# Expert tiles that add their rows to the residual stream, in place of a combine at the end

## What is computed

```python
t = rmsnorm(x, g_ffn)
g_logits, e_logits = t @ w_group + b_group, t @ w_router + b_router
g = argmax(g_logits)                       # one of 4 groups
top_v, top_i = top_k(e_logits[g], 2)       # 2 of its 4 experts
w = softmax(top_v) * softmax(g_logits)[g]
y = sum(w[k] * ((silu(t @ w_gate[e]) * (t @ w_up[e])) @ w_down[e]) for k, e in ...)
out = rmsnorm(x + y, g_final)
```

## Time and profile before

| | us |
|---|---|
| median of three runs (1074.95 to 1082.03) | 1076.79 |
| the profiled execution | 1083.94 |
| its span, first to last instruction | 1080.7 |
| routing, experts, combine | 69.5, 282.5, 59.7 |

### The profile page before, as it was taken

The page is one execution under the profiler, slowest core; times in us unless marked ns, Lnnn a source line. Parts: engine busy times, 40 slices in busy tenths (PEclk is TensorE's granted clock), DMA queues, the critical chain, the costliest instruction groups (busy, mean ns, idle before and its releaser), DMA issues. The chain is left out here.

```text
span 1080.7 us, 13980 instructions
## 1 busy us (share of the span) xinstructions
PE 943.3 (87%) x4765; PEld 764.4 (71%) x4765; DVE 431.6 (40%) x524; ACT 368.4 (34%) x544; POOL 128.6 (12%) x159
## 2 busy tenths in 40 slices
PE   6996999999999999989999997926999999989500
PEld 5785888888888676558888885715888887768400
DVE  4673212121211234232222232375646567675056
ACT  6762012111111123221122222503656567665212
POOL 0011000000001000000000001202112111211074
PEclk8997999999999999998999999965999999999855
DMA  9891101111005966544000102932587878993177
GB/s 384 329 297 60 49 1 39 40 40 40 20 20 210 408 262 279 203 182 161 1 1 1 29 1 76 331 118 79 196 309 260 307 260 317 341 337 131 69 268 259
DMA packets 37534, 181.38 MB, mean 168 GB/s; under 512 B 4268, under 2 KB 8748, under 8 KB 26811
## 3 DMA queue, kind: packets, MB, share of 16 engines
q1 hardware_dynamic: 26706, 141.57, 35.3%
q0 software_dynamic: 6864, 24.68, 7.2%
q10 hardware_dynamic: 3888, 14.16, 3.2%
HBM read 147.59 MB, written 40.78 MB: 174 GB/s over the span
## 5 line engine op out<-in xcount | busy, mean ns | idle before, releaser
L1634 DVE TENSOR_TENSOR Wl<-raw,Wh x48 | 109.9, 2292 | 72.9 <-ACT Wh L1574 72.8
L1574 ACT CAST Wh<-raw x48 | 91.6, 1911 | 55.4 <-issue 53.8
L1481 PE MATMUL ps<-Wh,e_xTh 128*128 x216 | 87.2, 404 | 4.0 <-issue 4.0
L551 PE MATMUL ps<-f_win_h,f_hTh 128*128 128x512 f32 x216 | 86.6, 401 | 0.6 <-DVE f_hTl L443 0.6
L1482 PE MATMUL ps<-Wl,e_xTh 128*128 x216 | 84.9, 393 | 0.0
L553 PE MATMUL ps<-f_win_l,f_hTh 128*128 128x512 f32 x216 | 84.8, 393 | 0.0
L1483 PE MATMUL ps<-Wh,e_xTl 128*128 x216 | 84.8, 393 | 0.0
L552 PE MATMUL ps<-f_win_h,f_hTl 128*128 128x512 f32 x216 | 84.5, 391 | 0.0
L1556 POOL DMA_INDIRECT e_xg<-h_rows,idx x28 | 46.7, 1669 | 247.0 <-PE ps L1666 199.3
L1481 PE MATMUL ps<-f_rg_h,f_cTh 128*128 128x512 f32 x144 | 56.7, 394 | 0.0
L1483 PE MATMUL ps<-f_rg_h,f_cTl 128*128 128x512 f32 x144 | 56.2, 390 | 0.0
(11 more groups left out here) (303 smaller groups left out, 1811.5 us busy)
## 6 DMA issues: line engine op xcount, KB each, us to landing
raw<-in_w_e SPq DMA_DIRECT2D x48, 1024.0 KB, 6.8
y_rows<-e_y ACTq DMA_DIRECT2D x27, 512.0 KB, 5.4
t_ring<-in_kc SPq DMA_DIRECT2D x8, 1024.0 KB, 12.5
t_ring<-in_vc SPq DMA_DIRECT2D x8, 1024.0 KB, 8.7
f_win_raw<-in_w_in SPq DMA_DIRECT2D x3, 2048.0 KB, 22.8
f_xin<-in_x SPq DMA_DIRECT2D x9, 512.0 KB, 3.6
x_rows<-f_xin SPq DMA_DIRECT2D x9, 512.0 KB, 2.6
y_rows<-in_x SPq DMA_DIRECT2D x1, 4608.0 KB, 19.8
```

Source lines behind the costliest of these rows:

```text
L551: pe.matmul(ps[:, bank, :], hTh[:, c, :], win_h[i][:, c, :], start=(c == 0), stop=False)
L1481: pe.matmul(out, xh, wh, start=(n == 0), stop=False)
L1574: act.copy(Wh[q][:, ds(off, PIECE)], raw[q][:, ds(off, PIECE)]).then_inc(hi_ok[q], 1)
L1634: dve.tensor_tensor(Wl[q][:, ds(off, PIECE)], raw[q][:, ds(off, PIECE)], Wh[q][:, ds(off, PIECE)].bitcast(F32), ALU.subtract).then_inc(lo_ ...
```

## The change

The combine goes. The stream is stored from `X` to `acc_rows` in DRAM at the end of routing. In the expert stage each tile gathers its rows of `acc_rows` (by the same `IDX`) into one of four slots `ring`; DVE adds `down`'s two halves to them out of PSUM; the weight of a pair (`GATE`) is already multiplied into `sg`. Rows that have one expert still to come are scattered back to `acc_rows` (`IDXR`), the others are squared by ACT, get their factor from POOL, are normed by DVE into `done` and scattered to the output `y` (`IDXF`). An index out of bounds drops a row, in the fetch too. To keep a row's two experts at least four tiles apart, the experts are numbered with the place in the group ahead of the group, and so are the weights in DRAM. The first four tiles have no norm. The last tile has its own tail: added, normed and scattered to `y` behind the loop. `xg` has three buffers instead of two and is filled with zeros by POOL at the start of routing; POOL's fetches run three tiles ahead.

The cut diff (the removed `combine_block`, declarations and host-side reshapes are left out):

```diff
-        for lo in range(MIN_TILES, NTILE, NT):
-            n = min(NT, NTILE - lo) * P
-            sp.dma_start(y_dram[lo * P:lo * P + n, :], io["x"][0:n, :]).then_inc(fill_st, 16)
-        sp.wait_ge(fill_st, 16 * -(-(NTILE - MIN_TILES) // NT))
...
@@ -1256,6 +1268,8 @@
                     for p in range(3):
                         sp.wait_ge(keep["w_ld"][p], 16 if n == 4 else 32)
                         load_piece(sp, io, keep, 1 if n == 4 else 2, p)
+            for n in range(NT):
+                sp.dma_start(acc_dram[n * P:(n + 1) * P, :], X[:, n, :]).then_inc(keep["acc_st"], 16)
             for b in range(XB):
...
         def _(pool):
             pool.memset(ones[:, :], 1.0).then_inc(ones_ok, 1)
+            pool.memset(keep["xg"][:, :, :], 0.0)
...
+                last = v(M[:, k, :, :].rearrange("p t (e g) -> p t e g", g=EG), bcast4(H[:, k, :, :], EG),
+                         G1[:, :, :].rearrange("p t (o g) -> p t o g", o=1).to_broadcast([P, NT, EE, EG]), ALU.mult)
             then(last)
             v(Ms[:, :, :], M[:, 0, :, :], M[:, 1, :, :], ALU.add).then_inc(M_ok, 1)
 
+
+            then(v(TK[:, 0, :], m["k1"][:, :], m["k2"][:, :], ALU.is_lt))
+            then(v(TK[:, 1, :], m["k2"][:, :], m["k1"][:, :], ALU.is_lt))
...
                 [P, K2, NTILE]), ALU.is_equal))
             for k in range(2):
-                last = v(A[:, k * NT:(k + 1) * NT, :], A[:, k * NT:(k + 1) * NT, :], bcast(tok[:, 0, :], NTILE), ALU.mult)
+                own = slice(k * NT, (k + 1) * NT)
+                then(v(A[:, own, 0, :], A[:, own, 1, :], bcast(TK[:, k, :], NTILE), ALU.mult))
+                last = v(A[:, own, 1, :], A[:, own, 1, :], bcast(WTr[:, k, :], NTILE), ALU.mult)
             last.then_inc(AB_ok, 1)
 
 
...
+            then(dve.tensor_scalar(none[:, :], val[:, :], 0.0, pad[:, :], ALU.is_equal, ALU.mult))
+            then(dve.scalar_tensor_tensor(out=none[:, :], in0=none[:, :], scalar=-1.0, in1=val[:, :], op0=ALU.add, op1=ALU.add))
+
+            dve.tensor_copy(IDX[:, :], none[:, :])
+            then(dve.scalar_tensor_tensor(out=val[:, :], in0=second[:, :], scalar=2 * LATER, in1=none[:, :], op0=ALU.mult,
+                                          op1=ALU.add))
+            then(dve.tensor_scalar(fin[:, :], second[:, :], -2 * LATER, 2 * LATER, ALU.mult, ALU.add))
+            dve.tensor_copy(IDXR[:, :], val[:, :])
+            then(v(fin[:, :], fin[:, :], none[:, :], ALU.add))
+            then(dve.tensor_copy(IDXF[:, :], fin[:, :]))
+            then(v(none[:, :], none[:, :], last_tile[:, :], ALU.mult))
+            then(r(used[:, 0:1], none[:, :], AX_X, ALU.add))
+            dve.tensor_copy(keep["idx_last"][:, :], used[:, 0:1])
 
 
 def split_product(pe, out, pairs):
...
+                if j >= XG:
+                    pool.wait_ge(tr_ps, j - XG + 1)
+                pool.indirect_dma_start(xg[:, j % XG, :], None, h_dram[:, :],
+                                        bass.IndirectOffsetOnAxis(ap=IDX[:, j:j + 1], axis=0), bounds_check=NT * P - 1, oob_is_err=False).then_inc(
+                    x_ld[j % XG], 16)
+
+            def gather(j):
+
+                if j >= EG:
+                    pool.wait_ge(y_st, 16 * (j - EG + 1))
                 else:
-                    with pool.If(started(pool, j - 1) >= 1):
-                        fetch(j)
+                    pool.wait_ge(acc_st, 16 * NT)
+                if j:
+                    pool.wait_ge(a_ld, 16 * j)
+                pool.indirect_dma_start(ring[:, j % 4, :], None, acc_dram[:, :],
+                                        bass.IndirectOffsetOnAxis(ap=IDX[:, j:j + 1], axis=0), bounds_check=NT * P - 1, oob_is_err=False).then_inc(a_ld, 16)
+
+            def scatter(j):
+                pool.wait_ge(y_ok, 2 * j + 2)
+                if j:
+                    pool.wait_ge(y_st, 16 * j)
+                pool.indirect_dma_start(acc_dram[:, :], bass.IndirectOffsetOnAxis(ap=IDXR[:, j:j + 1], axis=0),
+                                        ring[:, j % 4, :], None, bounds_check=NT * P - 1, oob_is_err=False).then_inc(y_st, 16)
+
+            def finish(j):
+
+                factors(j)
+                pool.wait_ge(f_ok, j - EG + 1)
+                if j > EG:
+                    pool.wait_ge(f_st, 16 * (j - EG))
+                pool.indirect_dma_start(io["y"], bass.IndirectOffsetOnAxis(ap=IDXF[:, j:j + 1], axis=0), done[:, j % 2, :],
+                                        None, bounds_check=SEQ + ROWS_S - 1, oob_is_err=False).then_inc(f_st, 16)
+
+            def factors(j):
+                c = 3 * (j % 2)
+                pool.wait_ge(sq_ok, SQ0 + j + 1)
+                pool.tensor_scalar(st[:, c + 1:c + 2], st[:, c:c + 1], 1.0 / D, EPS, ALU.mult, ALU.add).then_inc(r_ok, 1)
+                pool.wait_ge(r_ok, 2 * SQ0 + 2 * j + 1)
+                pool.tensor_tensor(st[:, c + 2:c + 3], st[:, c + 1:c + 2], nhalf[:, :], ALU.pow).then_inc(r_ok, 1)
+
+            pool.memset(factor[:, 0:1], 1.0 / D)
+            pool.memset(factor[:, 1:2], EPS)
+            for j in range(XG):
+                fetch(j)
+            with ExitStack() as maybe:
+                for s in range(NTILE):
+                    if s >= MIN_TILES:
+                        maybe.enter_context(pool.If(started(pool, s) >= 1))
+                    if s + XG - 1 < MIN_TILES:
+                        fetch(s + XG)
+                    elif s + XG < NTILE:
+                        with pool.If(started(pool, s + XG - 1) >= 1):
+                            fetch(s + XG)
+                    gather(s)
+                    if s >= 1:
+                        scatter(s - 1)
+                    if s > EG:
+                        finish(s - 1)
+
+            squares, before, every, added = squares_done(pool), sums(pool, 2), sums(pool, 3), sums(pool, 1)
+            pool.wait_ge(sq_ok, squares)
+            pool.tensor_tensor(mark[:, 1:2], mark[:, 0:1], factor[:, 0:1], ALU.mult).then_inc(mark_ok, 1)
+            pool.wait_ge(mark_ok, 1)
+            pool.tensor_tensor(mark[:, 1:2], mark[:, 1:2], factor[:, 1:2], ALU.add).then_inc(mark_ok, 1)
+            pool.wait_ge(mark_ok, 2)
+            pool.tensor_tensor(mark[:, 2:3], mark[:, 1:2], nhalf[:, :], ALU.pow).then_inc(mark_ok, 1)
+            pool.wait_ge(f_st, before)
+            pool.tensor_tensor(mark[:, 3:4], nhalf[:, :], nhalf[:, :], ALU.add).then_inc(mark_ok, 1)
+            pool.wait_ge(last_ok, 1)
+            pool.wait_ge(mark_ok, 4)
+            pool.indirect_dma_start(io["y"], bass.IndirectOffsetOnAxis(ap=keep["idx_last"][:, 0:1], axis=0), v_last,
+                                    None, bounds_check=SEQ + ROWS_S - 1, oob_is_err=False).then_inc(f_st, 16)
+
+            pool.wait_ge(f_st, every)
+            pool.tensor_tensor(mark[:, 3:4], nhalf[:, :], nhalf[:, :], ALU.add).then_inc(mark_ok, 1)
+            pool.wait_ge(y_st, added)
+            pool.wait_ge(mark_ok, 5)
+            pool.tensor_tensor(mark[:, 3:4], nhalf[:, :], nhalf[:, :], ALU.add).then_inc(mark_ok, 1)
 
         @block.scalar
         def _(act):
...
+            def square(j):
+                act.wait_ge(y_ok, 2 * j + 2)
+                act.wait_ge(sq_ok, SQ0 + j)
+                if j >= EG + 2:
+                    act.wait_ge(r_ok, 2 * (SQ0 + j) - 2)
+                    act.wait_ge(f_ok, j - EG - 1)
+                c = 3 * (j % 2)
+                act.activation(junk[:, :], ring[:, j % 4, :], ACT.Square, accum_out=st[:, c:c + 1]).then_inc(sq_ok, 1)
...
-                if like >= 1:
-                    par = (like - 1) % 2
-                    act.wait_ge(dn_ps, 2 * s - 1)
-                    if like >= 3:
-                        act.wait_ge(y_st[par], 8 * (s - 1 - par))
-                    act.copy(y[:, par, 0:512], ps[:, 4, :]).then_inc(y_ok, 1)
-                    act.wait_ge(dn_ps, 2 * s)
-                    act.copy(y[:, par, 512:D], ps[:, 5, :]).then_inc(y_ok, 1)
+                if like > EG:
+                    square(s - 1)
                 round_piece(s + 1, (2,))
-                if like >= 1:
-                    act.wait_ge(y_ok, 2 * s)
-                    act.dma_start(y_dram[ds((s - 1) * P, P), :], y[:, par, :]).then_inc(y_st[par], 16)
             tile_steps(act, step)
-
-            count = end(act, NE - 1)
-            stores = [act.value_load(TAB[0:1, 4, NE + par:NE + par + 1], min_val=16, max_val=8 * NTILE) for par in range(2)]
-            done = [tail(act, 1 + h) for h in range(2)]
-            act.wait_ge(y_st[0], stores[0])
-            for h in range(2):
-                act.wait_ge(dn_ps, done[h])
-                act.copy(y[:, 0, h * 512:(h + 1) * 512], ps[:, 4 + h, :]).then_inc(y_ok, 1)
-            act.wait_ge(y_ok, done[1])
-            act.dma_start(y_dram[ds((count - 1) * P, P), :], y[:, 0, :]).then_inc(y_st[0], 16)
-            act.wait_ge(y_st[0], stores[0] + 16)
-            act.wait_ge(y_st[1], stores[1])
-            act.copy(sg[0:1, 0:1], ident[0:1, 0:1])
+            every = tail(act, 2)
```

(36 more changed lines are left out.)

228 lines of the change are left out of this document (100 added, 128 removed).

## The result

The kernel before took 1080.12 us (median of 20 runs), the changed one 1074.53 us (median of 20): a ratio of 0.9947 with a 95% interval of 0.993 to 0.9963. That is a gain of 5.6 us where 20 were forecast. It is inside the range and within 1% of no change.

A forecast was written before the change was run, and what follows sets the result against it. PE was taken to bound the expert stage, with nothing running beside the 59.70 us combine. Terms -49.6 + 4.8 + 23 + 2 = -19.8 us took 1076.8 to 1057.0; range 1040 to 1068, 8 in 10 1036 to 1086.

The forecast's parts named there:

- behind the last matmul: End of the kernel: 59.7 us of combine shrink to a 10.1 us tail, -49.6 us.
- routing: Stage ahead of the experts: index path, index product, small operations behind it and POOL's fill add 4.8 us, bounds 3 and 8.
- first product to last: Expert stage, from first gate product on DVE to last: 250.75 us grow to 273.8, +23, bounds +9.5 and +31.
- 2 for the gather: Expert stage: a tile's gather is issued late in POOL's round and may land late, +2 us.
- step A: Expert step with two weight pieces on DVE: 9.9 with an early factor, 11.2 with a late one, 10.4 us taken.
- B: Expert step with one weight piece: additions, square, rounding, piece, norm, xTl and product in series, 10.3 us, nine of them.
- H: Expert step with three weight pieces: 11.3 us at least, 13.4 with a late factor, 12.9 taken, three with a norm.
- the first five: First five intervals between products, without a norm: three at PE's 9.3 us and two at 11, 49.9 together.
- The middle value: 10.4 us for a two-piece step, near the middle between POOL's scatter slipping ahead of the second piece and not.
- the rival that POOL is always late: Expert stage: every scatter generation meets a weight piece, stage +37 us, total -8, 1069 us; chance 0.15.
- Hidden work: Expert stage: PE keeps its pace because DVE catches up in one-piece steps; -45 us, 1032; chance 0.13.
- The round trip through memory: Expert stage: the loop of additions, scatter and gather binds; at 12.2 us per tile stage +55, total +11, 1088; chance 0.14.

The follow-up runs named there:

- round_early: Changed kernel with ACT's rounding of weight piece 0 of tile s+2 put ahead of the silu of tile s: 1061.57 us, 0.9833 of the kernel before.
- norm_next: Changed kernel with the norm of tile s-2 right behind the product of step s, its scatter to y one step later: 1047.62 us, 0.9705 of before.
- no_stream: Changed kernel without the gathers from and scatters to acc_rows in the expert loop: 1056.54 us, 0.9768 of the kernel before.
- factor_first: Changed kernel with POOL's two factor operations put ahead of the tile's scatter to acc_rows: 1056.94 us, 0.9791 of the kernel before.
- both: Changed kernel with the norm behind the next step's product and ACT's square behind the rounding of piece 2: 1041.79 us, 0.9635 of the kernel before.

## Why the prediction was right or wrong

The direction was right, the size was not: 20 us forecast, 5.6 measured. Against the sum's own terms, in the profiled executions:

| term | forecast | measured | from |
|---|---|---|---|
| behind the last matmul | -49.6 | -47.4 | 59.7 before, 12.3 now |
| routing | +4.8 | +3.7 | see below |
| ahead of routing | 0 | -2.4 | the same reduce of the attention ends 2.4 earlier |
| first product to last | +23, and 2 for the gather | +41.95 | 250.75, 292.70 |
| last product to last matmul | 0 | -1.9 | 13.65, 11.74 |
| sum | -19.8 | -6.1 | |

**The step that failed** is the cost of a step A, "9.1, under PE's 9.3" if the factor is early and "11.2" if it is late, from which 10.4 was taken. It measured 12.5. The working put the first piece right behind the product and left out the 1.81 us for which DVE waits there for ACT's rounding, though the earlier trace rows show that wait in the very row of 851.70. On the mean of the eight steps the rounding is waited for 1.84 us and the factor 1.83, and the rest of the step is 8.8, near the 9.1 of the sum: 10.4 left room for 1.3 us of waits where 3.7 were measured. The 11.2 has a slip besides: its 8.4 is counted from the start of the product, so the 0.41 at its end counts the product twice. Without that a late factor makes 10.8, and with the wait 12.6; with an early factor it is 10.9. Eight times 2.1 are 16.9 us, just what the stretch is off by. The others cancel, and that they do is luck (B +2.9, H -0.2, the first five -0.9, the last +0.2, no gather late -2). That the wait belongs to the chain is shown by `round_early`, which takes most of it away and 14.2 us with it, and by `norm_next`, which puts the norm into it and gains 24.

**The middle value was wrong as well.** The scatter was to slip ahead of the second piece half of the time. It never did: in all eight A steps the norm waited 1.83. The row that the argument rested on, a generation of 2.42 us that met a piece, was the right one; the rival that POOL is always late was the true case, at a chance of 0.15, with a size (+37 in the stage) nearer to the measured 42 than the forecast's. That size is partly luck: it had A at 11.2 to 12 and H at 13.4, without the wait for the rounding, where 12.5 and 12.8 were measured.

**B and H** were right: 10.3 forecast and 10.6 measured for B, where square, rounding, piece, norm and xTl stand in series, and 12.9 against 12.8 for H.

**Routing.** From one reduce of the attention (642.77 before, 640.38 now) to the first product it took 113.8 and now 117.5 us: +3.7 against +4.8. The index product with 64 columns cost 7.9 us as it had with 32, where 1 was counted; the chain behind it took 2.7 from 736.14 on, against the 2.4 counted.

**The end** took 12.3 instead of 10.1: both additions were exposed (1.29, not 0.68), and 2.4 us pass between POOL's last operation and the end of the span. The last scatter landed 2.6 us after its issue by the chain of waits, under the 4.2 that stood for it. It moved at most some 70 KB and not the 0.5 MB that the prediction counted, which fits a last tile with most of its places empty. The Trainium skill's 2.0 us plus bytes over 436 GB/s ("DMA: Bandwidth & Descriptors", Anatomy of one DMA) gives an estimate of 2.2 us for that much, and was nearer than the fetches.

**The rivals.** Hidden work fell: PE's pace was lost in A. The round trip through memory, the slower side, fell by `no_stream`, which without any of its traffic is no faster than `factor_first` with all of it. It exists, though: `norm_next` shows one tile that waited 3 us for a gather, and `both` one that waited 0.4. The rule that DVE and GpSimd hold a port for whole instructions ("SBUF — State Buffer", SBUF: two separate sides, of the Trainium skill) agrees with POOL's side where POOL begins second: generations of 2.6 us instead of 1.0, and a factor operation of 1.3 to 2.3 instead of 0.19. DVE's side doesn't show: with four generations per tile the pieces had a mean of 2289 ns, and 2292 before.
